# Two-layer hybrid attention block: the stacking of queries and keys laid out anew over DVE, POOL and ACT, with four tiles in flight

## The reference

```
def attend(q, k, v):
    s = jnp.einsum('bqhcd,bkhcd->bhcqk', q, k).astype(F32) * scale
    p = jax.nn.softmax(s, axis=-1)
    a = p[:, :, 0] - lam * p[:, :, 1]
    return jnp.einsum('bhqk,bkhd->bqhd', a, v.astype(F32))
```

## Time and profile before

| | |
|---|---|
| median of three runs | 2436.0 us |
| the profiled execution | 2436.36 us, of which the span of the engines' work is 2434.5 us |
| mean granted clock of TensorE | 0.92 of full |
| busy share of the span | PE 82%, DVE 56%, ACT 41%, POOL 21% |
| `stack_pair`, four calls, first cast to last copy | 18.79, 19.67, 18.80 and 19.07 us |

### The profile page before, as it was taken

The page is one execution under the profiler, slowest core; times in us unless marked ns, Lnnn a source line. Parts: engine busy times, 40 slices in busy tenths (PEclk is TensorE's granted clock), DMA queues, the critical chain, the costliest instruction groups (busy, mean ns, idle before and its releaser), DMA issues. The chain is left out here.

```text
span 2434.5 us, 37576 instructions
## 1 busy us (share of the span) xinstructions
PE 1991.5 (82%) x14664; PEld 1644.5 (68%) x14664; DVE 1354.4 (56%) x2539; ACT 991.0 (41%) x2056; POOL 499.9 (21%) x646
## 2 busy tenths in 40 slices
PE   4698798897767778898976987989987677788988
PEld 2587677786555657787854877878775565577767
DVE  2336527858878367322744256158488783573256
ACT  5233333334858436411225333232338684353111
POOL 1312315411010100322224214135120100002212
PEclk7899898898989889999997999989898898899999
DMA  9760250141000310313336720520330003202231
GB/s 366 231 183 19 61 165 19 40 108 28 1 1 1 117 57 1 87 52 114 120 132 239 215 70 21 144 79 3 98 76 1 1 1 106 67 1 70 69 121 52
DMA packets 68607, 203.26 MB, mean 83 GB/s; under 512 B 7856, under 2 KB 11216, under 8 KB 64720
## 3 DMA queue, kind: packets, MB, share of 16 engines
q0 software_dynamic: 38016, 93.34, 13.8%
q1 hardware_dynamic: 25232, 98.08, 11.3%
q10 hardware_dynamic: 5184, 9.44, 1.0%
HBM read 180.83 MB, written 19.92 MB: 82 GB/s over the span
## 5 line engine op out<-in xcount | busy, mean ns | idle before, releaser
L590 PE MATMUL ps<-ring_lo,h_hi 128*128 128x512 f32 (+3 forms) x800 | 269.2, 336 | 0.0
L590 PE MATMUL ps<-h_hi,ring_lo 128*128 128x512 f32 (+1 forms) x688 | 251.2, 365 | 0.0
L2164 DVE TENSOR_REDUCE a_st<-ps 128x1 f32<-128x1280 f32 (+1 forms) x144 | 196.7, 1368 | 44.3 <-PE ps L2049 44.1
L2117 ACT ACTIVATE ring<-ps,a_st 128x1280 f32<-128x1280 f32 (+1 forms) x144 | 177.4, 1232 | 55.8 <-DVE a_st L2164 55.5
L2049 PE MATMUL ps<-a_k,a_q 128*128 128x512 f32 (+1 forms) x400 | 126.1, 426 | 54.4 <-ACT ring L2117 50.0
L590 PEld LDWEIGHTS ps<-ring_lo,h_hi 128*128 128x128 f32 x800 | 156.6, 196 | 13.4 <-issue 1.0
L590 PE MATMUL ps<-h_hi,g_proj_wh 128*128 128x512 f32 (+1 forms) x400 | 149.1, 373 | 12.6 <-DVE ring_lo L560 7.7
L590 PE MATMUL ps<-g_proj_xl,g_proj_wh 128*128 128x512 f32 (+1 forms) x400 | 148.5, 371 | 0.0
L590 PEld LDWEIGHTS ps<-h_hi,ring_lo 128*128 128x128 f32 x688 | 130.4, 190 | 21.4
L2066 PE MATMUL ps<-cst,ring 128*128 128x128 f32 x656 | 104.7, 291 | 43.9 <-ACT ring L2126 18.4
L2049 PEld LDWEIGHTS ps<-a_k,a_q 128*128 128x128 f32 x400 | 73.4, 211 | 83.7 <-ACT ring L2117 67.1
(11 more groups left out here) (359 smaller groups left out, 5278.9 us busy)
## 6 DMA issues: line engine op xcount, KB each, us to landing
ring<-in_w SPq DMA_DIRECT2D x16, 2048.0 KB, 7.5
b_proj_xl<-h_low POOLq DMA_DIRECT2D x32, 640.0 KB, 4.3
a_proj_xl<-h_low POOLq DMA_DIRECT2D x64, 320.0 KB, 3.2
ring<-in_w SPq DMA_DIRECT2D x24, 512.0 KB, 3.7
b_proj_xl<-h_low POOLq DMA_DIRECT2D x32, 320.0 KB, 4.2
c_proj_xl<-h_low POOLq DMA_DIRECT2D x32, 320.0 KB, 3.2
d_proj_xl<-h_low POOLq DMA_DIRECT2D x32, 320.0 KB, 3.2
h_low<-h_low SPq DMA_DIRECT2D x32, 256.0 KB, 2.0
```

The source lines that it names most:

```text
L590: last = pe.matmul(out, left, right, start=k == 0 and j == 0, stop=k == KT - 1 and j == 2)
L2117: act.activation(p(u, c, n), ps[:, 3 * c:3 * c + 3, :].rearrange("p b n -> p (b n)")[:, 0:n], ACT.Exp, bias=st[:, 0:1], accum_out=st[:, 1: ...
L2164: dve.tensor_reduce(stat[:, u % SLOTS, c, 0:1], ps[:, 3 * c:3 * c + 3, :].rearrange("p b n -> p (b n)")[:, 0:n], AX.X, ALU.max, negate=Tru ...
```

## The change

Four things change in `stack_pair`, and nothing elsewhere.

- `hi`, `stack` and the PSUM banks get four slots instead of two (all eight banks are used).
- The queries' low part goes from DVE to POOL, which no longer copies the queries' high part.
- ACT lays out both high parts, two tiles ahead of its copies from PSUM instead of one.
- DVE casts three tiles ahead of its copies from PSUM and subtracts two tiles ahead.

The diff, without the lines that only rename the slots:

```
-            for t in range(NT):
-                if t >= 2:
-                    dve.wait_ge(high.sem, t - 1)
-                    dve.wait_ge(high_k.sem, t - 1)
-                    dve.wait_ge(turned.sem, t - 1)
-                dve.tensor_copy(hi[:, t % 2, :], src[:, t, :]).then_inc(split.sem, 1)
-                dve.wait_ge(split.sem, t + 1)
-                for s in range(2):
-                    dve.tensor_tensor(places(t, s, 1), maps(src[:, t, :], s), maps(hi[:, t % 2, :].bitcast(F32), s), ALU.subtract)\
-                       .then_inc(low.sem, 1)
-                if t >= 1:
-                    dve.wait_ge(turned.sem, t)
-                    dve.tensor_copy(k4[:, :, (t - 1) * P:t * P],
-                                    ps[:, 2 * ((t - 1) % 2) + 1, :].rearrange("p (m t) -> p m t", m=4)).then_inc(kept_k.sem, 1)
...
+            def split_tile(t):
+                if t >= SLOTS:
+                    dve.wait_ge(turned.sem, t - SLOTS + 1)
+                dve.tensor_copy(hi[:, t % SLOTS, :], src[:, t, :]).then_inc(split.sem, 1)
+
+            def low_k(t):
+                dve.wait_ge(split.sem, t + 1)
+                dve.tensor_tensor(places(t, 1, 1), maps(src[:, t, :], 1), maps(hi[:, t % SLOTS, :].bitcast(F32), 1), ALU.subtract)\
+                   .then_inc(low.sem, 1)
+
+            for t in range(3):
+                split_tile(t)
+                if t < 2:
+                    low_k(t)
             for t in range(NT):
+                if t + 3 < NT:
+                    split_tile(t + 3)
+                if t + 2 < NT:
+                    low_k(t + 2)
+                dve.wait_ge(turned.sem, t + 1)
+                dve.tensor_copy(k4[:, :, t * P:(t + 1) * P],
+                                ps[:, 2 * (t % 4) + 1, :].rearrange("p (m t) -> p m t", m=4)).then_inc(kept_k.sem, 1)
...
         def _(pool):
             for t in range(NT):
                 pool.wait_ge(split.sem, t + 1)
-                pool.tensor_copy(places(t, 0, 0), maps(hi[:, t % 2, :].bitcast(F32), 0)).then_inc(high.sem, 1)
+                if t >= SLOTS:
+                    pool.wait_ge(turned.sem, t - SLOTS + 1)
+                pool.tensor_tensor(places(t, 0, 1), maps(src[:, t, :], 0), maps(hi[:, t % SLOTS, :].bitcast(F32), 0), ALU.subtract)\
+                    .then_inc(low_q.sem, 1)
...
         def _(pe):
             for t in range(NT):
-                pe.wait_ge(low.sem, 2 * (t + 1))
+                pe.wait_ge(low.sem, t + 1)
+                pe.wait_ge(low_q.sem, t + 1)
                 pe.wait_ge(high.sem, t + 1)
-                pe.wait_ge(high_k.sem, t + 1)
-                if t >= 2:
-                    pe.wait_ge(kept_q.sem, t - 1)
-                    pe.wait_ge(kept_k.sem, t - 1)
+                if t >= 4:
+                    pe.wait_ge(kept_q.sem, t - 3)
+                    pe.wait_ge(kept_k.sem, t - 3)
...
         def _(act):
             def high_part(t):
                 act.wait_ge(split.sem, t + 1)
-                act.activation(places(t, 1, 0), maps(hi[:, t % 2, :].bitcast(F32), 1), ACT.Copy).then_inc(high_k.sem, 1)
-
-            high_part(0)
+                for s in range(2):
+                    last = act.activation(places(t, s, 0), maps(hi[:, t % SLOTS, :].bitcast(F32), s), ACT.Copy)
+                last.then_inc(high.sem, 1)
+
+            for t in range(2):
+                high_part(t)
             for t in range(NT):
-                if t + 1 < NT:
-                    high_part(t + 1)
+                if t + 2 < NT:
+                    high_part(t + 2)
```

More of the change, by code:

```diff
@@ L1908, in stack_pair @@
     ps, signal = env["ps"], env["signal"]
-    split, low, high, high_k, turned, kept_q, kept_k = (
-        signal(f"{name}_{n}") for n in ("stack_split", "stack_low", "stack_high", "stack_high_k", "stack_turned", "stack_q", "stack_k"))
+    split, low, low_q, high, turned, kept_q, kept_k = (
+        signal(f"{name}_{n}") for n in ("stack_split", "stack_low", "stack_low_q", "stack_high", "stack_turned", "stack_q", "stack_k"))
+    SLOTS = 4
     with ExitStack() as own, nc.Block() as block:
-        hi = own.enter_context(env["sbuf"](f"{name}_hi", [P, 2, 2 * P], F32R))
-        stack = env["ring"].rearrange("p a n -> p (a n)")[:, 0:2048].rearrange("p (u s m b c) -> p u s m b c", u=2, s=2, m=4, b=4)
+        hi = own.enter_context(env["sbuf"](f"{name}_hi", [P, SLOTS, 2 * P], F32R))
+        stack = env["ring"].rearrange("p a n -> p (a n)")[:, 0:SLOTS * 1024].rearrange("p (u s m b c) -> p u s m b c", u=SLOTS, s=2, m=4, b=4)
         def maps(x, s):
@@ L1920, in places @@
         def places(t, s, low):
-            x = stack[:, t % 2, s, :, :, :]
+            x = stack[:, t % SLOTS, s, :, :, :]
             return x[:, :, 2 * low:2 * low + 2, :] if s == 0 else x[:, :, low::2, :]
@@ L1925, in _ @@
         def _(dve):
-            for t in range(NT):
-                if t >= 2:
-                    dve.wait_ge(high.sem, t - 1)
-                    dve.wait_ge(high_k.sem, t - 1)
-                    dve.wait_ge(turned.sem, t - 1)
-                dve.tensor_copy(hi[:, t % 2, :], src[:, t, :]).then_inc(split.sem, 1)
-                dve.wait_ge(split.sem, t + 1)
-                for s in range(2):
-                    dve.tensor_tensor(places(t, s, 1), maps(src[:, t, :], s), maps(hi[:, t % 2, :].bitcast(F32), s), ALU.subtract)\
-                       .then_inc(low.sem, 1)
-                if t >= 1:
-                    dve.wait_ge(turned.sem, t)
-                    dve.tensor_copy(k4[:, :, (t - 1) * P:t * P],
-                                    ps[:, 2 * ((t - 1) % 2) + 1, :].rearrange("p (m t) -> p m t", m=4)).then_inc(kept_k.sem, 1)
-            dve.wait_ge(turned.sem, NT)
-            dve.tensor_copy(k4[:, :, (NT - 1) * P:NT * P], ps[:, 2 * ((NT - 1) % 2) + 1, :].rearrange("p (m t) -> p m t", m=4))\
-               .then_inc(kept_k.sem, 1)
+            def split_tile(t):
[10 more added lines that the diff above has]
+                    low_k(t)
+            for t in range(NT):
+                if t + 3 < NT:
[5 more added lines that the diff above has]
+                                ps[:, 2 * (t % 4) + 1, :].rearrange("p (m t) -> p m t", m=4)).then_inc(kept_k.sem, 1)
         @block.gpsimd
@@ L1953, in _ @@
             for t in range(NT):
-                pe.wait_ge(low.sem, 2 * (t + 1))
+                pe.wait_ge(low.sem, t + 1)
+                pe.wait_ge(low_q.sem, t + 1)
                 pe.wait_ge(high.sem, t + 1)
-                pe.wait_ge(high_k.sem, t + 1)
-                if t >= 2:
-                    pe.wait_ge(kept_q.sem, t - 1)
-                    pe.wait_ge(kept_k.sem, t - 1)
+                if t >= 4:
+                    pe.wait_ge(kept_q.sem, t - 3)
+                    pe.wait_ge(kept_k.sem, t - 3)
                 for s in range(2):
                     for m in range(4):
-                        last = pe.transpose(ps[:, 2 * (t % 2) + s, m * P:(m + 1) * P],
-                                            stack[:, t % 2, s, m, :, :].rearrange("p b c -> p (b c)"), C(env, "ident"))
+                        last = pe.transpose(ps[:, 2 * (t % 4) + s, m * P:(m + 1) * P],
+                                            stack[:, t % SLOTS, s, m, :, :].rearrange("p b c -> p (b c)"), C(env, "ident"))
                 last.then_inc(turned.sem, 1)
@@ L1969, in high_part @@
                 act.wait_ge(split.sem, t + 1)
-                act.activation(places(t, 1, 0), maps(hi[:, t % 2, :].bitcast(F32), 1), ACT.Copy).then_inc(high_k.sem, 1)
-            high_part(0)
+                for s in range(2):
[3 more added lines that the diff above has]
+                high_part(t)
             for t in range(NT):
-                if t + 1 < NT:
-                    high_part(t + 1)
+                if t + 2 < NT:
+                    high_part(t + 2)
                 act.wait_ge(turned.sem, t + 1)
-                act.activation(q4[:, :, t * P:(t + 1) * P], ps[:, 2 * (t % 2), :].rearrange("p (m t) -> p m t", m=4), ACT.Copy)\
+                act.activation(q4[:, :, t * P:(t + 1) * P], ps[:, 2 * (t % 4), :].rearrange("p (m t) -> p m t", m=4), ACT.Copy)\
                    .then_inc(kept_q.sem, 1)
```

## The result

The changed kernel takes 2411.88 us (median of four runs, 2411.13 to 2414.74) against 2436.12 us for the kernel before (four runs, 2428.62 to 2441.05): the ratio is 0.990, with a 95% interval of 0.9878 to 0.9922. That is 24.2 us less, where 22 were forecast. The profiled execution took 2411.13 us, its span is 2409.3 us.

A forecast was written before the change was run, and what follows sets the result against it. DVE's own work, 1.79 us a tile, was taken to bound the four `stack_pair` calls. Savings of 24.4 us (ACT as end) or 20.6 (DVE) gave a middle of 22.5: 2436.4 to 2414 us, range 2405 to 2427.

The forecast's parts named there:

- The stretch and its limit: Four `stack_pair` calls between barriers, 76.33 us together, limited by DVE, busy 71.56; savings there reach the end, 22.5 us.
- DVE's sum: DVE's casts, key subtractions and PSUM copies per call: 11.7 us (12.1 with waiting for first transposes) or 13.7.
- The 0.20 on the keys' subtraction: Keys' subtraction on DVE, 0.54 against 0.34 us: goes if POOL's interference, stays if due to short runs.
- the upper value (13.7): DVE's call length in us if the key subtraction stays at 0.54; 20.6 us saved over four calls.
- Fill and drain hardly change: Start and end of each call: first transposes at the same time as before, first copies 2.47 us after first cast.
- one of the prediction's own signs of being wrong: In the calls, a DVE cast or key subtraction of 0.9 us or more would point to POOL taking the port.
- ACT's sum: ACT's twenty high parts at 0.35 and ten PSUM copies at 0.53 per call: 12.7 us.
- the better case: ACT ends the calls at 12.7, 13.6, 12.7 and 13.0 us; 24.4 us saved.
- its 0.88: POOL's subtraction per tile: 0.62 plus 0.26 us for broken pattern or DVE's presence; 0.6 to 0.9 taken, hidden.
- Rival A: POOL takes the port first each tile, DVE waits its whole instruction: about 3 us saved, or up to 2448; chance 0.07.
- Rival C: Clock falls to half level in half of each call, giving 8 us back: 2422; chance 0.19 shared with another rival.
- The gain of clock behind the calls: Low-clock stretches behind the calls partly recover: 5 to 10 us more saved, 2406; chance 0.08.

The follow-up runs named there:

- pool_memset: Changed kernel with POOL filling the queries' low part with zeros by memset instead of subtracting; calls 13.3 to 13.4 us, median 2409.86 us.
- memset_warm: Changed kernel with POOL's memset of zeros instead of its subtraction, plus ten added PE transposes at each call's start; calls 12.1 us, total 2406.17 us (one run).
- copy_first: Changed kernel with DVE's copy from PSUM put before the keys' subtraction; period 1.30 us, calls 15.1 to 15.4 us, median 2416.69 us.
- warm_pe: Changed kernel with ten identity transposes added on PE at each call's start; calls 13.4 us, total 2408.3 us (one run).
- after_again: Changed kernel unaltered, run a second time; calls 13.6 to 13.9 us, median 2413.32 us.
- first_and_warm: Changed kernel with the queries' low part of tiles 0 and 1 on DVE and ten added PE transposes; calls 13.0 to 13.1 us, median 2410.99 us.
- both_again: Same kernel as first_and_warm, run again beside after_again; calls 13.0 to 13.1 us, median 2414.45 us.
- first_on_dve: Changed kernel with the queries' low part of tiles 0 and 1 subtracted on DVE, POOL starting at tile 2; calls 13.0 to 13.5 us, median 2415.9 us.

## Why the prediction was right, and where it was off

- *The stretch and its limit.* The four calls, bounded by DVE's own list, were the place: 21.9 us saved in them against 22.5 forecast. Beside them nothing shows that is larger than the scatter of several microseconds.
- *DVE's sum.* Both terms in doubt were settled. The 0.20 on the keys' subtraction was POOL's interference and went, so the steady period is 1.14, the lower of the two values. The prediction halved the difference to the upper value (13.7), and 13.6 was measured, but not for that reason: the interference came back in another place, the start. Casts of neighbouring tiles are 1.14 apart, under the 1.2 to 1.35 that the prediction looked for.
- *The start of a call.* "Fill and drain hardly change" failed: the first copy comes 3.70 us after the first cast, not 2.47. There the casts stand next to POOL's first subtractions, with no copy from PSUM between, and three instructions are held for 0.54 each. pool_memset and memset_warm show it: without POOL's reads they take their plain time, and at full clock a call takes 12.1 us. A key subtraction of 0.9 us or more was one of the prediction's own signs of being wrong; it came (0.96), once a call.
- *ACT's sum.* The term was over-sized: a pair of layouts costs 0.62, not 0.70, and a copy 0.47, not 0.53, so ACT needs 1.09 a tile instead of 1.23, and its sum is 11.3 us instead of 12.7. It was forecast as the end in the better case; DVE was the end in fact, busy 13.42 of 13.60 us. The over-sized ACT, the half of DVE's upper value and the missing 1.6 us of held instructions cancelled: 12.7 by ACT became 12.1 plus 1.5 by DVE. That was luck. With every other term right and the hold left out, the sum at full clock would be the 12.1 of memset_warm, 28 us saved instead of 22.5; with the clock at half near the start, for which the prediction allowed in two of the four calls, it would be the 13.3 of pool_memset.
- *POOL.* 0.85 us in mid-call, inside the 0.6 to 0.9 taken, and hidden; the first two of a call take 0.96, a little above. The prediction built its 0.88 from a costly pattern or DVE's presence; both are in it, 0.73 for the pattern when nothing of DVE's is in the way and 0.12 for DVE's subtraction.
- *Rival A, the port.* It was right that order decides and that a tile in steady state is spared, as copy_first shows: 0.16 a tile once the order is turned. Its mechanism was at work, but in three instructions of each call instead of in all ten tiles, and a held instruction cost 0.54, the part of POOL's 0.96 that was still to come, not the whole of it. The Trainium skill, "SBUF — State Buffer", section "Who interferes with whom", has the rule that a DVE instruction with two SBUF inputs contends with a GpSimd instruction that reads SBUF and not with one that only writes it, that a DVE instruction in a two-port mode, which a cast can enter, contends with GpSimd, and that the one issued first keeps the shared pair for the whole instruction. The traces here agree for the subtraction (0.96 against 0.42 beside POOL's subtraction, 0.42 beside its memset) and for the cast (0.82 against 0.28 beside POOL's subtraction); in which mode the cast runs no run here shows.
- *Rival C, the clock.* The clock fell in every call, to 0.87 on average, with the half level near the start, and cost 0.2 us a call (warm_pe), up to 0.5 in two calls of after_again, as DVE covered most of it. The gain of clock behind the calls, which the rival allowed for, did not come: from the first call's end to the second's start it was 103.2 us before and 104.8 after, and from the third's to the fourth's 95.5 and 95.4, in one trace of each.
- *The total.* 24.2 us against 22, of which the traces find 21.9 in the calls; the rest is within the scatter.

## What to carry to other kernels

Sum each engine's list from start to start, and treat the first tiles apart: what overlaps harmlessly in the steady state may collide there. Work moved from DVE to POOL was free here where DVE had issued its own subtraction first or was copying out of PSUM; where POOL's subtraction was issued first, DVE's casts and subtractions waited for its end. The order of two independent instructions decided it. Deeper buffering and a shorter list on the bounding engine gave 7.8 and 5.4 us alone and 21.9 together, so neither alone tells what the pair is worth.

## What the runs showed of the hardware

- A DVE cast from SBUF to SBUF is held by POOL as long as a subtraction is: 0.82 us instead of 0.28 beside a POOL subtraction, 0.96 instead of 0.42 for the subtraction.
- The hold goes both ways. POOL's subtraction takes 0.73 us with nothing in its way, 0.85 to 0.97 where a DVE subtraction came first, and up to 1.19 where it met a cast and then a subtraction (first_and_warm).
- Ten transposes of a constant in PE's idle time ahead of a call went with a granted clock at full in three of four calls in warm_pe and in all twelve of first_and_warm, both_again and memset_warm; in the changed kernel without them PE stood idle for 2.5 us there, and the clock was at half for part of the first 6 us of all eight calls in two traces. Idleness alone doesn't explain it: in the kernel before PE idled 2.4 us at the same place, and the clock stayed at full in the first and third call; it did in one call of first_on_dve too. What decides stays open.
- ACT's copies overlap what follows by more than the 0.07 us read from one pair: 0.59 us of duration cost 0.47.
